# A fused two-block transformer kernel: in the mixers, the attention's steps placed behind a weight unit go ahead of the convolution's taps

## The reference, cut to what matters

```python
def mixer_block(h, ...):                       # h: 256 x 1024
    u = h @ w_in
    u_conv, q, k, v, u_pool, gates = split(u)
    y_conv = conv_branch(u_conv)               # glu, 31-tap depthwise conv, layer norm, silu, @ conv_pw
    y_attn = diff_attention(q, k, v) @ attn_o  # 8 heads, two softmax maps a head, per-head rms norm
    y_pool = pool_branch(u_pool)               # windowed means, @ pool_w, @ pool_o
    g = sigmoid(gates)
    return (g0 * y_conv + g1 * y_attn + g2 * y_pool) @ w_out
```

## Time and profile before

| | us |
|---|---|
| median of 3 runs | 2358.39 |
| lowest, highest | 2355.55, 2358.86 |
| the profiled execution, its own time | 2359.51 |
| its span, first to last instruction | 2357.7 |

### The profile page before, as it was taken

How to read it: one execution, slowest core, us unless ns; L and a number is a source line. 1 busy time by engine, 2 the same in 40 slices (tenths; PEclk the granted TensorE clock), 3 DMA queues, 4 the chain that set the end, 5 groups by cost and what they waited for, 6 DMA issues and landing times.

```text
span 2357.7 us, 43891 instructions
## 1 busy us (share of the span) xinstructions
PE 2252.8 (96%) x18003; PEld 2155.7 (91%) x18003; DVE 1709.2 (72%) x2733; ACT 1179.4 (50%) x1843; POOL 91.7 (4%) x86
## 2 busy tenths in 40 slices
PE   6998999999999999989999999999999989999998
PEld 5976899999999997889898999999998889898998
DVE  6766887887675798887655764775897887665764
ACT  2665445774544533555544544544533555535543
POOL 1000000110010000000000010010000000000110
PEclk7998999999999999999999999999999999999999
DMA  8634575667566653345553766566653345463754
GB/s 241 204 111 134 161 245 174 187 187 248 166 200 188 208 177 111 114 139 175 165 179 108 208 192 193 177 205 187 198 180 103 117 137 186 134 197 101 222 177 137
DMA packets 399911, 405.11 MB, mean 172 GB/s; under 512 B 18182, under 2 KB 392312, under 8 KB 399713
## 3 DMA queue, kind: packets, MB, share of 16 engines
q1 hardware_dynamic: 396177, 389.27, 54.0%
q0 software_dynamic: 3536, 13.04, 1.8%
HBM read 401.17 MB, written 1.09 MB: 171 GB/s over the span
## 4 chain that ended last, share of the span: by engine, by line
PE 71%; DVE 19%; ACT 5%; issue 4%; DMA 1%; DVEq 0%; POOL 0%; ACTq 0%; POOLq 0%
PE gemm_ps L962 46%; PE gemm_ps L965 16%; DVE weights_lo L1592 6%; DVE x_res L2058 4%; PE misc_ps L1103 2%; PE misc_ps L1104 2%; DVE mod_partial L1691 1%; ACT weights_hi L1219 1%; ACT e L1386 1%; DVE h_lo L1730 1%; PE misc_ps L1136 1%; PE misc_ps L1100 1%; DVE neg_max L1818 1%; DVE y L1766 1%; PE misc_ps L1121 1%
## 5 line engine op out<-in xcount | busy, mean ns | idle before, releaser
L1592 DVE TENSOR_TENSOR weights_lo<-raw_weights,weights_hi 128x1024 fp32r<-128x1024 f32 x704 | 835.6, 1198 | 375.1 <-ACT weights_hi L1219 371.4
L1219 ACT CAST weights_hi<-raw_weights 128x1024 fp32r<-128x1024 f32 x704 | 717.1, 1032 | 627.1 <-PE gemm_ps L962 428.4
L962 PE MATMUL gemm_ps<-h_hi,weights_hi 128*128 128x256 f32 x3280 | 930.0, 284 | 12.5 <-DVE h_lo L1730 3.5
L962 PE MATMUL gemm_ps<-h_lo,weights_hi 128*128 128x256 f32 x3280 | 914.3, 279 | 0.0
L962 PE MATMUL gemm_ps<-h_hi,weights_lo 128*128 128x256 f32 x3280 | 913.9, 279 | 0.0
L962 PEld LDWEIGHTS gemm_ps<-h_hi,weights_hi 128*128 128x128 f32 x3280 | 621.0, 189 | 21.1 <-issue 14.8
L962 PEld LDWEIGHTS gemm_ps<-h_lo,weights_hi 128*128 128x128 f32 x3280 | 621.9, 190 | 3.4 <-issue 3.0
L962 PEld LDWEIGHTS gemm_ps<-h_hi,weights_lo 128*128 128x128 f32 x3280 | 620.0, 189 | 0.0
L2058 DVE SCALAR_TENSOR_TENSOR x_res<-zp,param_cols,x_res 128x256 f32<-128x256 f32 x480 | 196.4, 475 | 0.0
L965 PE MATMUL gemm_ps<-weights_hi,hidh 128*128 128x256 f32 x688 | 189.9, 276 | 0.0
L965 PE MATMUL gemm_ps<-weights_hi,hidl 128*128 128x256 f32 x688 | 189.9, 276 | 0.0
(11 more groups left out here) (326 smaller groups left out, 3128.6 us busy)
## 6 DMA issues: line engine op xcount, KB each, us to landing
raw_weights<-in_ffn_w_dram SPq DMA_DIRECT2D x256, 512.0 KB, 4.4
raw_weights<-in_w_in_dram SPq DMA_DIRECT2D x200, 512.0 KB, 3.9
raw_weights<-in_w_mod_dram SPq DMA_DIRECT2D x48, 512.0 KB, 4.8
raw_weights<-in_w_up_dram SPq DMA_DIRECT2D x44, 512.0 KB, 4.5
raw_weights<-in_xattn_kv_dram SPq DMA_DIRECT2D x32, 512.0 KB, 4.4
raw_weights<-in_w_out_dram SPq DMA_DIRECT2D x24, 512.0 KB, 4.5
raw_weights<-in_w_down_dram SPq DMA_DIRECT2D x20, 512.0 KB, 4.5
raw_weights<-in_w_branch_dram SPq DMA_DIRECT2D x16, 512.0 KB, 4.5
```

Of the source, the lines that this page charges most:

```text
L962: mm = pe.matmul(ps[:, c, 0:T], w[:, m, kt, c * P:(c + 1) * P], x[:, f, :], start=start, stop=stop_)
L1219: act.copy(unit_of(WH, m % SPLIT, u), unit_of(RAWB, u["raw"] % RAW, u)).then_inc(sems["weights_rounded"], 1)
L1592: dve.tensor_tensor(unit_of(WL, m % SPLIT, u), unit_of(RAWB, u["raw"] % RAW, u), unit_of(WH, m % SPLIT, u), ALU.subtract).then_inc(sems["w ...
```

## The change

`spread` gets a parameter `attention_first` in place of `late`, which no call used. With it, no slot is placed while the next step of `main` is one of the attention's; so the slot goes behind the last of them. The number of slots behind a unit, and the unit, stay as they were. The outer call in `mixer` sets it.

```diff
-    def spread(main, slots, evac_first=lambda kind, k: False, late=False):
+    def spread(main, slots, evac_first=lambda kind, k: False, attention_first=False):
 
@@
-            if late and following[0] != "unit":
+            if attention_first and following[0] in ("scores", "turn", "softmax", "pv", "subln"):
                 continue
             while put < len(slots) * seen // n:
@@
-        S.extend(spread(main + last[:half], conv(range(0, NF, 2))))
+        S.extend(spread(main + last[:half], conv(range(0, NF, 2)), attention_first=True))
```

## The result

| | before | after |
|---|---|---|
| median, us | 2358.39 (5 runs) | 2369.94 (5 runs) |
| lowest, highest | 2355.55, 2359.52 | 2364.28, 2371.51 |
| ratio after to before, 95% interval | | 1.0045 [1.0027, 1.0063] |
| the profiled execution's own time | 2359.51 | 2364.28 |
| its span | 2357.7 | 2362.5 |

The change costs 11.55 us between the medians, 0.49%, and 10.7 us between the means, which is the 0.45% of the ratio. The profiled execution of after is the quickest of its five, so its trace shows the smaller part of the loss. Landmarks in the two timelines of TensorE say where that part is. They are the first `scores` of each mixer (L1103) and the first matmul of the mean behind it (L1171).

The account below looks back on a forecast made before the run. The prediction took TensorE, busy 96%, as the bound, with VectorE's queue order counting only where TensorE waits. Its terms -1.0 + 4.7 + 4.3 + 3.0 = +11.0 us on 2358.39 gave 2369.4 us, range 2361 to 2377.

Parts of the forecast that it names:

- Moves that are moves, and the price of one: Eight swaps per layer in VectorE's queue count, other queues cost 0; six taps in front delay what follows by 2.37 us.
- Swaps behind a softmax or pv: Six of the eight swaps: TensorE's short waits for exps before unit 305, scores1 and scores5 vanish, -1.0 us.
- Turn7: Turn7 comes 2.37 us earlier, but unit 334 then waits for evac_branch, which stands behind the taps in both orders: 0.
- Rival (c): Not slower: unit 334 not held by evac_branch, so turn7's gain reaches TensorE; -1.6 us, 2356.8 us; chance 0.08.
- subln1: Unit 314: taps now behind L1879, which waits for the root; unit 318 comes 2.37 us later per layer, +4.7 us.
- subln3: Unit 322: taps behind L1879 delay head 5's exps, so scores6 waits 2.12 and 2.14 us in the layers, +4.3 us.
- The clock: One short stretch of TensorE at the lower clock behind each scores6, 1.5 us each, +3.0 us.
- The wait of L1879: Sign in the changed profile: its wait for the root grows from 15.0 us in 8 by 4 times 2.37 to about 24.5.
- Rival (b): No change, 2358.4 us: VectorE, idle 28% of the span, takes up the moved 2.37 us; chance 0.12 together with (d).
- Rival (d): The swaps don't take place as read, for instance taps already behind the subln's unit; 2358.4 us; chance 0.12 with (b).
- Rival (a): Worse by the clock: both upper bounds, at scores6 and at unit 314's scores4, 18.0 us in sum, 2376.4 us; chance 0.10.

## Why the prediction was right

It said 2369.4 us, 0.47% slower; the median is 2369.94, 0.49% slower, or 0.45% by the ratio. The waits behind the subln swaps are shown. That the total comes within 0.6 us is luck in part: the clock's term isn't shown in its size, one median of five executions can move by some us, and a subln term that was too large stands beside a clock term that may be too small. By its own steps:

- **Moves that are moves, and the price of one.** Six taps take 2.37 us, and the delays found behind a multiply are 2.38 us and less, as long as TensorE keeps its clock. GpSimd's wait behind TensorE's turns is 489.1 us in all against 488.0, and the loads of weights land as before (3.9 us for those of `w_in`, 4.4 for `ffn_w`, in both). Right.
- **Swaps behind a softmax or pv, -1.0 us.** The waits before scores1 and scores5 are gone from the timeline; the kernel that keeps only these swaps (and the pv ones) is at 0.9991 [0.9973, 1.0010], which holds the -1.0 us and also zero.
- **Turn7, 0.** Right in amount and in cause: 1.79 + 2.45 us for 4.17 in layer 0, 1.69 + 2.45 for 4.16 in layer 1, and with taps behind evac_branch the 2.45 disappears. Rival (c) is refuted by that.
- **subln1, +4.7 us.** Unit 318 is 2.38 us later against the multiply in both layers, as forecast, and alone the swap cost 4.7 us [0.5, 8.7]. The profiles of the kernels with both subln swaps alone and with subln1's alone add what this term left out: in layer 0 scores4 runs at the lower clock there, and unit 318 is 2.92 us later (14.07 instead of 11.15).
- **subln3, +4.3 us.** The mechanism is right, the size a little too large: scores6 waits 1.79 and 1.70 us, 3.5 in all, instead of 2.12 and 2.14. The term `2.37 - 0.25` was mis-sized: the step took the queue behind the multiply for unbroken. In fact `lo` (L1592) waited there 0.19 and 0.18 us for ScalarE's rounding, and the taps now stand in that time. These are the lines of VectorE before, in both layers:

```profile
988.67 1.23 DVE L1592 TENSOR_TENSOR weights_lo<-raw_weights,weights_hi 128x1024 fp32r<-128x1024 f32 x1 [0.19 <-ACT weights_hi L1219]
...
1862.42 1.23 DVE L1592 TENSOR_TENSOR weights_lo<-raw_weights,weights_hi 128x1024 fp32r<-128x1024 f32 x1 [0.18 <-ACT weights_hi L1219]
```

From the start of the multiply to the start of this `lo` it is 3.05 and 3.04 us after, instead of 0.94, so 2.11 and 2.10 more and not 2.37. The slack of about 0.25 us that the forecast took off was right. From the multiply to scores6 it is 991.34 - 984.34 = 7.00 us instead of 992.89 - 987.73 = 5.16, so 1.84 more, and 1.86 in layer 1.
- **The clock, +3.0 us.** Chosen with bounds from 0 to 10. The trace of after shows none of it behind scores6, so that sign failed in this execution; its one longer stretch is at unit 334 in layer 0. In the kernels with subln3's swap alone and with both subln swaps there is such a stretch behind scores6 in both layers, of 6.8 us and once 10.2, and not 3.4. By the waits measured, -1.0 + 4.8 + 3.5 = 7.3; of the 10.7 us between the means that leaves 3.4 for the clock and scatter together, of the 11.55 between the medians 4.3. That fits the 3.0 and doesn't show it: the interval of the ratio goes from 6.4 to 14.9 us. The mean granted clock, 0.9788 against 0.9824, would be worth up to 8.5 us, as an estimate; what of it fell where TensorE waits anyway costs nothing. So the clock may have cost more than its term, and its share stays open.
- **The wait of L1879, forecast 24.5 us.** 22.5 us was measured in after, 29.7 with the subln swaps alone, the extra there mostly at subln3 of layer 0 (5.83 us) and at the two subln5. The forecast took each of four to grow by 2.37. At subln1 it did, by 2.31 and 2.38; at subln3 it grew by 0.59 and 1.98 only. In layer 0 VectorE ends the `lo` ahead of that multiply 3.51 us behind the end of scores5 in the kernel before, and 5.29 us behind it in after: 1.78 us later against TensorE, which is the 2.37 - 0.59. The forecast had let VectorE arrive there as early as before, although it carries work over from subln1. What counts for the time is what stands behind the multiply, and that moved by 2.38 us at unit 318 and by 2.10 at `lo`.

Rival (b) is refuted: VectorE is idle 28% of the span and the delay reached TensorE all the same. The Trainium skill (Perfetto Trace Analysis, Identifying the Most-Contended Engine) has one optimize the engine with the highest occupancy first. Here TensorE's is 96% in all these kernels with the same 18003 matmuls, and the order of an engine that is busy 72% is worth from +0.57% to -0.56%. So the rule names the engine whose gaps count, and can't say alone that a change elsewhere is free. Rival (d) is refuted by the timelines. Rival (a) needed both upper bounds in one execution; its 2376.4 lies above the highest run of after, 2371.51. It is not far-fetched: with the same subln swaps alone two of six executions took 2376.66 and 2378.58 us, and the latter's trace shows the low clock round scores4 and behind both scores6 that (a) describes.

## What to carry to other kernels

Where an engine works its queue in order, as VectorE does here, independent work put ahead of an instruction that waits for another engine was free as long as the wait lasted. The same work behind it was paid by everyone who waits further down the queue, less the slack on the way: of a tap step of 2.37 us, all arrived at unit 318 and 1.84 us at scores6. So for each wait ask how long the engine stands there, and fill that time from below; the gain came from four places, two a layer, where VectorE had stood 3.33 and 1.60 us, and not from the order of the steps in general. Putting work off behind an evacuation moves the debt to the next wait: sum the waits of the whole stretch before believing a gain at one of them.

## What had not been expected of the hardware

- ScalarE loads a table for Ln (L1223) and another for the Exp right behind it (L1225), 1.28 us each and 17 times each in the program. The Trainium skill (ScalarE: Activation LUTs, Table sets: the hidden batching unit) gives one load for this pair, since one set holds both; the trace disagrees for the kernel as written, and agrees once that set is loaded ahead by hand: then neither Ln nor Exp in these roots has a load. The loads don't vanish: ScalarE has 1841 instructions instead of 1843, since the set is loaded eight times ahead of the roots, and the table of the gates' Tanh (L1480) eight times instead of twice. They only leave the chain.
- The Trainium skill (ScalarE: Activation LUTs, What ACT_TABLE_LOAD costs) gives 1283 ns for the load and about as much again for a drain, some 2.66 us a switch. The 1283 ns is what the trace has; of the drain nothing shows here, as the load starts 0.02 us behind the end of the copy before it and the Ln starts 944.35 - 943.06 - 1.28 = 0.01 us behind its load.
- The lower clock followed waits of TensorE of only 1.69 and 1.77 us, when scores came behind them, with subln3's swap alone, and in the kernel after the same place, with 1.79 and 1.70 us, kept 2.4 GHz. So gaps of the same length were followed by either level. What decides it stays open; that it makes part of the scatter is an inference.
